# P of the sliding-window attention copied by DMA and transposed in one pass, with the second head of each pair scaled by ScalarE

## The reference

```
def block(args):                      # n = one of the blocks of 128 queries
    scores = einsum('bqhgd,bkhd->bhgqk', qn, keys) - slopes * dist
    m = maximum(max(scores, axis=-1), sink)
    p = exp(scores - m)
    probs = p / (sum(p, axis=-1) + exp(sink - m))
    return einsum('bhgqk,bkhd->bqhgd', probs, vals)     # 16 heads of 64
```

## Time and profile before

| | us |
|---|---|
| median of 3 runs | 1620.01 (1619.48 to 1620.28) |
| profiled execution: span, first to last instruction | 1618.2 |
| outside the span, median less span | 1.8 |
| PE busy | 1610.1 (99%) |
| PE weight loads busy | 1347.5 (83%) |
| DVE busy | 1030.6 (64%) |
| ACT busy | 769.9 (48%) |
| POOL busy | 437.1 (27%) |

### The profile page before, as it was taken

One profiled execution on the slowest core, in us unless ns is written; L12 is line 12 of the kernel. 1 busy time (PEld: TensorE's weight loads), 2 busy tenths in 40 slices (PEclk: granted clock), 3 DMA queues, 4 the chain that ended last, 5 costly groups with the idle time before them and its releaser, 6 DMA issues.

```text
span 1618.2 us, 22594 instructions
## 1 busy us (share of the span) xinstructions
PE 1610.1 (99%) x7984; PEld 1347.5 (83%) x7984; DVE 1030.6 (64%) x1913; ACT 769.9 (48%) x1567; POOL 437.1 (27%) x675
## 2 busy tenths in 40 slices
PE   9999999999999999999999999999999999999999
PEld 6888888888888888888888888888888888888887
DVE  6775556655657676757565338866665657766675
ACT  6533334545547676763222126655545544444442
POOL 1101010221359888875221000121111122100000
PEclk9999999999999999999999999999999999999999
DMA  8323232645424343438553223344444399733452
GB/s 289 116 98 117 95 124 72 232 166 186 162 88 114 84 94 83 106 82 262 164 202 104 72 65 124 129 170 150 149 144 148 119 321 356 239 98 98 149 183 92
DMA packets 119599, 236.53 MB, mean 146 GB/s; under 512 B 13904, under 2 KB 48128, under 8 KB 119488
## 3 DMA queue, kind: packets, MB, share of 16 engines
q0 software_dynamic: 45904, 126.93, 23.6%
q1 hardware_dynamic: 73440, 108.03, 21.6%
q10 hardware_dynamic: 144, 0.13, 0.0%
HBM read 157.05 MB, written 69.47 MB: 140 GB/s over the span
## 4 chain that ended last, share of the span: by engine, by line
PE 97%; DVE 1%; DMA 1%; ACT 0%; SPq 0%; POOL 0%; issue 0%; DVEq 0%; ACTq 0%
PE bank L1084 29%; PE bank L1089 29%; PE bank L1088 29%; PE bank L1370 2%; PE bank L1402 2%; PE bank L1384 2%; PE bank L1419 0%; PE bank L1127 0%; PE bank L1502 0%; PE bank L1288 0%; PE bank L1406 0%; PE bank L1452 0%; DMA PX<-in_w_in 0%; PE bank L1387 0%; DVE WL L2172 0%; PE bank L1427 0%
## 5 line engine op out<-in xcount | busy, mean ns | idle before, releaser
L1084 PE MATMUL bank<-WH,ADH 128*128 128x512 f32 x448 | 174.3, 389 | 0.0
L1088 PE MATMUL bank<-WH,ADL 128*128 128x512 f32 x448 | 174.3, 389 | 0.0
L1089 PE MATMUL bank<-WL,ADH 128*128 128x512 f32 x448 | 174.3, 389 | 0.0
L1084 PE MATMUL bank<-HN,WH 128*128 128x512 f32 x384 | 152.4, 397 | 0.0
L2098 ACT CAST ADH<-ARAW 128x512 fp32r<-128x512 f32 x112 | 69.5, 621 | 169.9 <-PE bank L1089 160.9
L1089 PE MATMUL bank<-HN,WH 128*128 128x512 f32 x384 | 150.3, 391 | 0.0
L1088 PE MATMUL bank<-HN,WL 128*128 128x512 f32 x384 | 150.0, 391 | 0.0
L959 POOL TENSOR_SCALAR PR<-PR,RC 128x272 f32<-128x272 f32 (+1 forms) x128 | 131.0, 1099 | 44.9 <-DVE RC L2663 44.4
L2917 DVE TENSOR_TENSOR ADL<-ARAW,ADH 128x512 fp32r<-128x512 f32 x112 | 77.5, 692 | 96.9 <-ACT ADH L2098 96.7
L1084 PE MATMUL bank<-SOPH,WH 128*128 128x512 f32 x256 | 99.8, 390 | 0.0
L1089 PE MATMUL bank<-SOPL,WH 128*128 128x512 f32 x256 | 99.6, 389 | 0.0
(11 more groups left out here) (356 smaller groups left out, 4242.8 us busy)
## 6 DMA issues: line engine op xcount, KB each, us to landing
ARAW<-uop SPq DMA_DIRECT2D x112, 256.0 KB, 3.0
uop<-US POOLq DMA_DIRECT2D x64, 256.0 KB, 2.8
WRAW<-in_w_up SPq DMA_DIRECT2D x15, 1024.0 KB, 6.2
RAW<-in_w_in SPq DMA_DIRECT2D x58, 256.0 KB, 4.0
gates<-TB POOLq DMA_DIRECT2D x48, 256.0 KB, 2.4
uop<-UA POOLq DMA_DIRECT2D x48, 256.0 KB, 3.1
proj<-SA POOLq DMA_DIRECT2D x36, 256.0 KB, 2.5
RT<-proj POOLq DMA_DIRECT2D x8, 1024.0 KB, 8.8
```

What stands on the lines that cost most here:

```text
L1084: mm = pe.matmul(bank, ahi, bhi, start=first, stop=False, skip_group_check=onto)
L1088: pe.matmul(bank, alo, bhi, start=False, stop=False, skip_group_check=onto)
L1089: return pe.matmul(bank, ahi, blo, start=False, stop=last, skip_group_check=onto)
```

## The change

P is no longer transposed out of PR. A DMA on SP's queue (`copy_p`) copies the two heads' P of a pair, 544 columns, into a new tile PW of type float32r with two places; PE transposes from PW with the float32r identity IDR. For this:

- `LAG = 3`: the transposes of a pair stand three steps behind its scores (two before), and there are 68 steps (67 before). `values` now falls in odd steps, and the meta part of `take_p` and `lo_p` in even ones.
- on PE the transposes of the next Q and K stand before those of P, so that all one-pass transposes of a step are next to each other.
- POOL scales the first head alone. ACT scales the second head of pair T-1 with `scale_second`, its first instruction in step T, which waits for `rc_rdy`, DVE's reciprocal of that pair.
- the sink columns are written by DVE, between `lo_p` and the scores, and no longer by POOL; that copy waits for the DMA of pair T-3.
- to make room, K and V keep four places (`NKV`) and not eight, with later loads, and weight tiles 4 and 5 of three slabs go to a tile of their own (RAWA). SP's loads of weights get fixed steps.

```diff
-STEPS = NPAIR + 3
+LAG = 3
+STEPS = NPAIR + LAG + 1
...
+        RAWA = at("RAWA", O_M + 8192, [2, SL])
+        PW = at("PW", O_M + 12288, [2, 2 * NKEY], F32R)
...
+            def copy_p(pair):
+
+                n, b = pair // 8, pair % 2
+                lo, hi = (0, 2 * NKEY) if n else (P, P + 2 * NKEY0)
+                sp.wait_ge(pn_rdy, pair + 1)
+                sp.wait_ge(pa_rdy, PA1 + pair + 1)
+                if pair >= 2:
+                    sp.wait_ge(pt_full, pair - 1)
+                sp.dma_start(PW[:, b, lo:hi].bitcast(F32), PR[:, pair % 3, 1 + lo:1 + hi]).then_inc(pw_full[b], 16)
...
             for T in range(STEPS):
...
+                if 1 <= T < NPAIR + 1:
+                    copy_p(T - 1)
...
             for T in range(STEPS + 2):
-                if T + 1 < NPAIR:
-                    set_sink(T + 1)
                 if 1 <= T <= NPAIR:
                     b = (T - 1) % 3
                     pool.wait_ge(rc_rdy, T)
-                    for hl in range(2):
-                        keys = PR[:, b, pr_keys((T - 1) // 8, hl)]
-                        pr = pool.tensor_scalar(keys, keys, RC[:, b, hl:hl + 1], None,
-                                                ALU.mult)
-                    pr.then_inc(pn_rdy, 1)
+                    keys = PR[:, b, pr_keys((T - 1) // 8, 0)]
+                    pool.tensor_scalar(keys, keys, RC[:, b, 0:1], None, ALU.mult).then_inc(pn_rdy, 1)
...
             def transpose_p(pair):
-                n, b = pair // 8, pair % 3
-                pe.wait_ge(pn_rdy, pair + 1)
+                n, b = pair // 8, pair % 2
+                pe.wait_ge(pw_full[b], PW0 + 16 * (pair // 2 + 1))
...
-                        pe.transpose(B[4][:, c * P:(c + 1) * P], PR[:, b, key:key + P], IDN[:, :])
+                        c, key = 2 * sl + hl, pr_slot(n, hl, sl) - 1
+                        pe.transpose(B[4][:, c * P:(c + 1) * P].bitcast(F32R), PW[:, b, key:key + P], IDR[:, :])
...
+            def scale_second(pair):
+                act.wait_ge(rc_rdy, pair + 1)
+                keys = PR[:, pair % 3, pr_keys(pair // 8, 1)]
+                act.activation(keys, keys, ACT.Copy, scale=RC[:, pair % 3, 1:2]).then_inc(pa_rdy, 1)
+
             for T in range(STEPS):
+                if 1 <= T <= NPAIR:
+                    scale_second(T - 1)
                 for i in gate_steps(T):
...
                 if T >= 3:
-                    dve.wait_ge(pt_full, T - 2)
+                    dve.wait_ge(pw_full[(T - 3) % 2], PW0 + 16 * ((T - 3) // 2 + 1))
+                if T == 0:
+                    dve.wait_ge(d_set, 1)
+                first, second = sink_at(n, 0), sink_at(n, 1)
+                dve.tensor_copy(PR[:, T % 3, first:second + 1:second - first], NSK[:, 2 * p:2 * p + 2]).then_inc(sk_set, 1)
                 for hl in range(2):
```

More of the change, by code:

```diff
@@ L682, in load_next @@
+            def load_next(slab, k):
+                sp.wait_ge(w_ready, wn(slab - 1, k if k >= 2 else k + 6) + 1)
+                if k >= 2:
                     sp.wait_ge(raw_full[raw_slot(slab - 1, k + 2)], raw_count(slab - 1, k + 2))
                 sp.dma_start(RAW[:, raw_slot(slab, k), :], w_from[slab - SLAB_D](k)).then_inc(raw_full[raw_slot(slab, k)], 16)
[L685 to L689, removed]
@@ L691, in _, with load_aside @@
-            for T in range(STEPS):
[L692 to L704, removed]
+            def load_aside(slab, k):
+                if slab > SLAB_D + 1:
+                    sp.wait_ge(w_ready, wn(slab - 1, k) + 1)
+                sp.wait_ge(raw_full[raw_slot(slab, k)], raw_count(slab, k - 2))
+                sp.dma_start(raw_block(slab, k), w_from[slab - SLAB_D](k)).then_inc(raw_full[raw_slot(slab, k)], 16)
@@ L709, in _ @@
                     load_block(8 * SLAB_D + 11)
+                if T == 1:
+                    sp.wait_ge(o_full, NB + START)
+                if T in (1, 2):
+                    load_aside(SLAB_D + 1, T + 3)
+                elif T in (22, 24):
+                    load_aside(SLAB_D + 2, 4 + (T - 22) // 2)
+                elif T in (40, 42):
+                    load_aside(SLAB_D + 3, 4 + (T - 40) // 2)
                 for slab, k in new_slabs(T):
                     if slab < SLAB_E and k in (0, 1):
[L712 to L715, removed]
+                        load_late(slab, k + 6)
+                if T < 60 and T % 20 in (10, 12, 14, 16):
+                    load_next(SLAB_D + 2 + T // 20, (2, 3, 0, 1)[(T % 20 - 10) // 2])
+                if NPAIR - 4 <= T < NPAIR:
+                    k = T - NPAIR + KT
                     sp.wait_ge(a_free, ACT_D + 28)
-                    for k in range(4, KT):
-                        sp.dma_start(raw_block(SLAB_E, k), w_from[SLAB_E - SLAB_D](k)).then_inc(uraw[k // 6], 16)
+                    sp.dma_start(raw_block(SLAB_E, k), w_from[SLAB_E - SLAB_D](k)).then_inc(uraw[k // 6], 16)
             def load_branch(m):
@@ L968, in _ @@
                     pool.dma_start(DT[:, n % 2, :], c_dist[n]).then_inc(dt_full[n % 2], 16)
-                if T in (5, 13, 21, 37):
-                    n = min(T // 8, 3)
-                    pool.wait_ge(qh_rdy, 3 * n + 3 if n else 2)
+                if T % 8 == 4 and 2 <= T // 8 < 6:
+                    n = T // 8 - 2
+                    pool.wait_ge(pv_full, 4 * (n + 2))
                     pool.wait_ge(qf_rdy, n + 2)
[L973 to L977, removed]
+                    load_kv(n + NKV)
+                if T >= LAG + 4 and T % 2 == 1:
+                    G = (T - LAG - 4) // 2
                     pool.wait_ge(yc_done[G % 2], 32 * (G // 2 + 1) + (16 if G % 2 else PL0))
@@ L1433, in _ @@
                     gate_step(i)
-                if T >= 4 and T % 2 == 0:
-                    values((T - 4) // 2)
-                if 2 <= T < NPAIR + 2:
-                    transpose_p(T - 2)
+                if T >= LAG + 2 and T % 2 == 1:
+                    values((T - LAG - 2) // 2)
                 if T in NEXT_Q:
@@ L1941, in _ @@
                         g.then_inc(a_free if c < 16 else th_rdy, 1)
[L1942 to L1945 removed]
+                if LAG <= T < NPAIR + LAG:
+                    take_p(T - LAG)
+                if T >= LAG + 2 and T % 2 == 1:
+                    take_y((T - LAG - 2) // 2)
                 if T % 8 == 2 and T // 8 + 1 < NB:
@@ L2675, in _ @@
                         split_lo(slab, k)
-                if T > NPAIR:
+                if T > NPAIR + 1:
                     for slab, k in new_slabs(T):
                         split_lo(slab, k)
-                if T >= NPAIR and T < NPAIR + 2:
+                if NPAIR + 1 <= T < NPAIR + 3:
                     for b in range(4):
-                        lo_ys(4 * (T - NPAIR) + b, b, T - NPAIR)
-                splits = new_slabs(T) if T < NPAIR else []
+                        lo_ys(4 * (T - NPAIR - 1) + b, b, T - NPAIR - 1)
+                splits = new_slabs(T) if T <= NPAIR else []
                 if T % 8 == 0 and T // 8 + 1 < NB:
```

79 lines of the change are left out of this document (36 added, 43 removed).

## The result

| | kernel before | kernel after |
|---|---|---|
| time, median (us) | 1620.14 (1619.48 to 1620.54, 4 runs) | 1629.78 (1628.86 to 1630.34, 4 runs) |
| span of the profiled execution | 1618.2 | 1628.1 |
| ratio after / before | | 1.0058, 95% interval 1.0044 to 1.0071 |

The change made the kernel slower by 0.6%. The forecast was 1632 us (range 1619 to 1643): the direction is right, the size 2.2 us too large.

The account below looks back on a forecast made before the run. PE bounds the kernel before; after the change a ring of ACT and DVE does in the attention loop. Span 1618.2 with -1.3 + 12.7 - 1.8 + 2.5 gives 1630.3, plus 1.8 to the median: 1632 us, range 1619 to 1643.

Parts of the forecast that it names:

- a ring of ACT and DVE: Attention loop: PTH, PTL, scores' maximum, exponentials, reciprocal, now closed by the scaling; 4.37 us a step against 4.00 for PE.
- The transposes' gain: On PE: 304 transposes of P, each 0.018 us cheaper in float32r, 5.5 us, lost whole once PE is not the bound.
- The bare round: Attention loop: 3.43 us from PTH to the reciprocal's end plus 0.60 for handover, scaling and sink copy, 4.03 us.
- the handover: Way from DVE's reciprocal to ACT's scaling in each round, taken as 0.09 us.
- What comes to it: Added to the loop's 55 rounds: tanh 10.6 us, late reciprocals 3 us, bursts 5 us.
- late reciprocals and bursts: DVE working longer than ACT's exponentials, 3 us; weight splits and normalising delaying PTL or an exponential, 5 us (0 to 10).
- the lead: Loop's start: the maximum is ready 2 us before its waiting scores start; PE stands still only after that, -1.8 us.
- The ends: Outside the loop: -1.3 us up to the scores of step 8, +2.5 us behind the last scores.
- PE as the bound: Rival for the attention loop: PE still sets the pace, the loop gives 5.5 + 0.5 us back, 1614 us; chance 0.09.
- The ring at its low bounds: Rival for the loop: the ring closes with only 0.47 us added a round and no bursts, 1620 us; chance 0.10.
- The late copy: Rival: P's copy on SP's queue lands late, DVE's sink copy waits, 28 us more, 1660 us; chance 0.06.
- The change doesn't make the transposes cheaper: Rival on PE: transposes stay at 0.108 us; with the ring as bound still 1632 us, no case of its own.

Follow-up runs that it names:

- the kernel before that gets the ring alone: Kernel before, with ACT scaling the second head first in the next step and POOL only the first; no copies, lag 2, float32 transposes: 1625.60 us.
- the experiment: Kernel after with the sink columns written by POOL again, as before, and no longer by DVE: 1626.05 us, ratio 1.0038.

## Why the prediction came out as it did

- **PE stops being the bound; a ring of ACT and DVE takes over: shown.** By the place of the scaling (1629.78 against 1614.82 with the same work), by the dearer transposes that cost 0.6 us in the one and 4.7 us in the other (0.1 and 5.0 us of the loop), and by the kernel before that gets the ring alone. The wait for PE at PTH is gone and the wait for RC is 0.32 us a step, where "about 0.3" stood.
- **The transposes' gain of 0.018 us each, lost whole: right.** 5.0 us over 275 in the loop where PE is the bound, 0.1 us in the kernel after.
- **The bare round: mis-sized.** A bare round is one without a tanh and without late work on DVE. Forecast 4.03 us, measured (3.77 + 3.20) / 2 + 0.46 = 3.945 us in steps 20 and 21. The scaling holds ACT for 0.43 us (546.61 to 547.04), as taken, and the sink copy DVE for 0.07 (544.59 to 544.66; 0.065 by the experiment), where 0.08 was taken. The term that was mis-sized most is the handover: 0.09 us was read at a maximum that ACT waits for; from the reciprocal's end to the scaling it is 0.03 (546.58 to 546.61). That is 0.06 of the 0.085 us. Over 55 rounds 217.0 us for the 221.9 that stood: 4.9 too much.
- **What comes to it: 1.5 us too little.** The tanh's 0.48 us each is seen (0.94 for 0.46). Of 235.3 us, 217.0 are bare rounds (55 x 3.945) and 10.6 the tanh; 7.7 are left for late reciprocals and bursts less the lead, for which 3 + 5 - 1.8 = 6.2 stood. The timelines of ACT and DVE take this apart. From the PTH at 488.03 to the one at 724.54 the ring makes its 55 rounds in 236.5 us, some 9 more than bare rounds and tanh: 8 ahead of the reciprocal, nearly all in 18 rounds, and 1 behind it, where a weight split stands ahead of the scaling. PE's count of the loop is 1.2 us shorter; that much of the lead was used up. So 9 us stand for the 8 forecast, and 1.2 for 1.8. In the longest of these rounds DVE is still busy with QNF and a weight split when the second exponential is through, and the reciprocal starts 1.53 us behind that exponential's start (663.08), where 0.64 is the quiet distance:

```profile
662.80 1.29 DVE L2564 TENSOR_TENSOR QNF<-RT,RSW 128x512 f32<-128x512 f32 x2
664.01 0.68 DVE L2183 TENSOR_TENSOR WL<-RAW,WH 128x512 fp32r<-128x512 f32 x1
664.61 0.16 DVE L2678 RECIPROCAL RC<-RS 128x2 f32<-128x2 f32 x1
```

- **The loop:** +7.5 us, where 12.7 - 1.8 = 10.9 was said: 4.9 less for the rounds and 1.5 more for the rest.
- **Luck in the total:** 1632 is only 2.2 us above the measured time because errors of opposite sign met: the rounds were 4.9 us too dear, and the rest of the loop, the ends and the remainder of the program together 2.7 us too cheap.
- **The ends:** -1.5 for -1.3 at the start, +3.1 for +2.5 behind. The rest of the program, costed at nothing, took 0.8 us more; the cause of this stays open.
- **Where PE stands still: named wrong.** The prediction let PE wait for `nm_rdy` at the scores. The trace has no row there; PE stands at `values` (L1406, 5.8 us in 14 waits), and for 1.3 us in 4 waits at the transposes for the low part, which the prediction named as the other place. One place of the kernel after, PE and then DVE:

```profile
547.90 0.39 PE L1093 MATMUL bank<-HN,WH 128*128 128x512 f32 x1
548.44 0.47 PE L1406 MATMUL bank<-PTH,KVR 128*128 128x512 f32 x1 [0.15 <-issue]
```

```profile
547.64 0.69 DVE L2653 TENSOR_TENSOR PTL<-bank,PTH 128x512 fp32r<-128x512 f32 x1 [1.06 <-ACT PTH L1913]
```

  The matmul starts 0.54 us behind the one ahead of it, where 0.23 is the distance of two such, and 0.11 us behind the end of PTL (547.64 + 0.69 = 548.33). The low part comes late, since PTH does. The profile writes "issue" for it. By the program `values` waits for `pl_rdy`, the low part; that this is what ends the wait is read from the times, and no run showed it by itself.
- **PE's busy share: too low.** 92 to 95% was said, 96.6% is there. Matmuls' busy times cover part of a wait, as the row above shows: PE is 0.31 us late, and 0.15 of it is counted as idle.
- **The copy in time: right.** PE never waits for it in the kernel after. It lands in 2.9 us (part 6 of the page), quicker than the weight loads from which the estimate was made, 256 KB in 4.0 us. The page writes 272 KB for its 278,528 bytes, which the prediction called 278 KB:

```profile
PW<-PR SPq DMA_DIRECT2D x56, 272.0 KB, 2.9
```

- **The rivals.** PE as the bound (1614 forecast) is what the kernel is once the scaling stands behind PTH, 1614.82. The ring at its low bounds (1620) was near with its round, 3.90 for 3.945 measured, but wrong to take the bursts at nothing: with them late work adds 9 us, where it had 3. The late copy did not occur. "The change doesn't make the transposes cheaper" is refuted by the pair with float32 transposes; that the time would hardly depend on it holds (1630.35 against 1629.78).
- **Two slips in the working.** The upper end of the range doesn't follow from its terms: 4.37 + (0.78 - 0.60) is 4.55 us a step and 1642 us, not 4.57 and 1643. And the 0.16 us a transpose beside the four passes comes from no row of this case: three times the 0.090 us of a one-pass transpose would be 0.27, 82 us. The 1632 rests on neither.

## What to carry to other kernels

Before a waiting instruction is put first into an in-order engine's step, follow what it waits for once round: if that comes from work behind the same instruction of the last step, the sum of the round, handovers and small copies included, is a bound of its own, and it is to be compared with the step of the busiest engine. Here 3.95 us, with the tanh and the bursts 4.28, stood against 4.03 of PE, while ACT was busy for only 76% of the loop. The remedy is one line further down: behind the instruction that closes the round, the same work cost nothing that could be measured, and only then did the cheaper transposes show (1614.8 us, for 1620 before).

## What the runs showed of the hardware beyond what was expected

- A copy of two columns on DVE is shown as 0.15 to 0.43 us long, but the next instruction starts 0.06 to 0.08 us behind its start; in the ring it costs 0.065 us. Distances between starts, not durations, make up a round.
- From DVE to ACT the way is 0.03 us behind the shown end of the reciprocal and 0.09 us behind that of the reading of the maximum; over the loop of the kernel after, 0.02 to 0.04 and 0.09 to 0.10 us, in some 50 waits of each kind: a handover is to be read at the same kind of instruction.
- Four float32r transposes go in 0.34 us between those of Q and that of the meta columns, 0.085 us each, for 0.108 in float32 (PE of the kernel after):

```profile
545.05 0.51 PE L1388 MATMUL bank<-IDR,PW 128*128 128x128 f32 x4
545.39 0.25 PE L1391 MATMUL bank<-IDR,PW 128*128 128x128 f32 x1
```

  "FP8 and Floating Point Precision" of the Trainium skill (TensorE Precision Notes) gives true float32 four passes; a transpose shows nothing like it here: 0.108 us against 0.085, and in the pair of experiments 0.018 us each and not three passes more.
- "ScalarE: Activation LUTs" of the Trainium skill (What ACT_TABLE_LOAD costs) gives an ACTIVATE 186 ns, 0.833 ns a column and 93 ns for a pointer operand, with 93 ns of overlap behind another: by it, as estimates, 506 ns for the scaling, 392 for half of it, and 186 for the second instruction. The trace agrees within 4% on the durations, with 525 and 403 ns; the second instruction costs less than the estimate, 0.17 us a round.
